# The third feed-forward quarter in two sets of seven block products, with the residual kept in DRAM

## What is computed

```python
def swiglu(x, w_gate, w_up, w_down):
    return (jax.nn.silu(x @ w_gate) * (x @ w_up)) @ w_down

h = h + 0.5 * rmsnorm_2(swiglu(u, ff1_w_gate, ff1_w_up, ff1_w_down), ff1_post_g)   # and again with ff2
```

## Time and profile before

| | us |
|---|---|
| median of three runs | 2805.66 |
| lowest and highest of them | 2805.01, 2805.68 |
| span of the profiled execution | 2803.9 |
| TensorE busy in it | 2789.1 |
| VectorE busy in it | 2219.1 |
| ScalarE busy in it | 1485.1 |

### The profile page before, as it was taken

One profiled execution on the slowest core, in us unless ns is written; L12 is line 12 of the kernel. 1 busy time (PEld: TensorE's weight loads), 2 busy tenths in 40 slices (PEclk: granted clock), 3 DMA queues, 4 the chain that ended last, 5 costly groups with the idle time before them and its releaser, 6 DMA issues.

```text
span 2803.9 us, 34346 instructions
## 1 busy us (share of the span) xinstructions
PE 2789.1 (99%) x13154; PEld 2329.8 (83%) x13154; DVE 2219.1 (79%) x2554; ACT 1485.1 (53%) x1747; POOL 14.5 (1%) x20
## 2 busy tenths in 40 slices
PE   9999999999999999999999999999999999999998
PEld 8888888888898888888888888888888888888887
DVE  6869757865565888889888877687799888889885
ACT  5544545554544555555455555755655555555564
POOL 0000000000000000000000000000000000000000
PEclk9999999999999999999999999999999999999999
DMA  7546355555545555655655558543665656565654
GB/s 250 202 155 199 112 182 190 186 189 180 165 150 197 196 193 197 206 199 199 202 196 194 196 165 270 177 160 125 204 200 189 203 187 208 197 204 198 204 187 158
DMA packets 276010, 530.71 MB, mean 189 GB/s; under 512 B 8769, under 2 KB 32465, under 8 KB 275393
## 3 DMA queue, kind: packets, MB, share of 16 engines
q1 hardware_dynamic: 274864, 527.01, 56.6%
q0 software_dynamic: 752, 2.04, 0.2%
q10 hardware_dynamic: 288, 0.20, 0.0%
HBM read 527.12 MB, written 2.10 MB: 189 GB/s over the span
## 4 chain that ended last, share of the span: by engine, by line
PE 97%; DVE 1%; DMA 0%; ACT 0%; issue 0%; SPq 0%; DVEq 0%; ACTq 0%
PE ps L817 19%; PE ps L818 19%; PE ps L820 17%; PE ps L1373 10%; PE ps L1375 9%; PE ps L1374 9%; PE ps L826 2%; PE ps L902 1%; PE ps L901 1%; PE ps L900 1%; PE ps L845 1%; PE ps L846 1%; PE ps L850 1%; PE ps L1081 1%; PE ps L1367 1%; PE ps L1061 1%
## 5 line engine op out<-in xcount | busy, mean ns | idle before, releaser
L2450 DVE TENSOR_TENSOR w_lo<-raw,w_hi 128x2048 fp32r<-128x2048 f32 (+4 forms) x301 | 663.0, 2206 | 193.9 <-ACT w_hi L1683 193.1
L1683 ACT ACTIVATE w_hi<-raw 128x2048 fp32r<-128x2048 f32 (+4 forms) x301 | 555.1, 1849 | 259.5 <-DMA raw<-in_ff_w_down 107.4
L817 PE MATMUL ps<-w_hi,x_hi 128*128 128x512 f32 (+4 forms) x1760 | 679.1, 386 | 1.7 <-ACT z L1716 0.7
L818 PE MATMUL ps<-w_lo,x_hi 128*128 128x512 f32 (+4 forms) x1760 | 669.5, 380 | 0.0
L820 PE MATMUL ps<-w_hi,x_lo 128*128 128x512 f32 (+4 forms) x1536 | 582.7, 379 | 0.0
L817 PEld LDWEIGHTS ps<-w_hi,x_hi 128*128 128x128 f32 x1760 | 330.7, 188 | 62.6 <-issue 2.3
L818 PEld LDWEIGHTS ps<-w_lo,x_hi 128*128 128x128 f32 x1760 | 330.9, 188 | 58.6
L820 PEld LDWEIGHTS ps<-w_hi,x_lo 128*128 128x128 f32 x1536 | 288.4, 188 | 53.3
L2217 ACT ACTIVATE w_hi<-raw 128x1024 fp32r<-128x1024 f32 x156 | 164.9, 1061 | 278.4 <-DMA raw<-in_ff_w_up 144.7
L1373 PE MATMUL ps<-w_hi,x_hi 128*128 128x512 f32 x780 | 305.4, 392 | 0.1
L1375 PE MATMUL ps<-w_hi,x_lo 128*128 128x512 f32 x780 | 303.8, 389 | 0.0
(11 more groups left out here) (486 smaller groups left out, 4019.4 us busy)
## 6 DMA issues: line engine op xcount, KB each, us to landing
raw<-in_w_in SPq DMA_DIRECT2D x139, 1024.0 KB, 5.1
raw<-in_ff_w_gate SPq DMA_DIRECT2D x88, 1024.0 KB, 5.2
raw<-in_ff_w_up SPq DMA_DIRECT2D x88, 1024.0 KB, 5.3
raw<-in_ff_w_down SPq DMA_DIRECT2D x88, 1024.0 KB, 5.1
raw<-in_w_out SPq DMA_DIRECT2D x45, 1024.0 KB, 5.2
raw<-in_w_ple_gate SPq DMA_DIRECT2D x16, 1024.0 KB, 5.0
raw<-in_w_in SPq DMA_DIRECT2D x8, 696.0 KB, 4.3
raw<-in_w_in SPq DMA_DIRECT2D x8, 520.0 KB, 3.8
```

What stands on the lines that cost most here:

```text
L817: nc.tensor.matmul(o, x[0][:, k0 + c, s], hi[:, c, 0:width], start=first and c == 0, stop=False)
L818: nc.tensor.matmul(o, x[0][:, k0 + c, s], lo[:, c, 0:width], start=False, stop=False)
L1683: nc.scalar.activation(landed_part(w_hi, u, j), landed_part(raw, u, j), ACT.Copy).then_inc(hi_ready, 1)
L2450: V.tensor_tensor(landed_part(w_lo, u, j), landed_part(raw, u, j), landed_part(w_hi, u, j).bitcast(F32), ALU.subtract).then_inc(parts_read ...
```

## The change

Block i = 0 keeps its three sets. In the blocks i = 1 to 9 quarter 2 (`DOUBLE`) is done wholly in two sets of seven, so that a block has five sets: (0,0), (1,0), (2,0), (2,1), (3,0). The sums of activations for the new set (`half_xs`, lower and upper part) are made once in block 0, in memory of attention masks.

The sums now are four chunks apart from the units: up - gate for both chunks in one instruction of 1024 columns (`first_sums`), then two of 512. There is a second place for them in the memory of `res`, used by the sets (1,0) and (2,1) from block 1 on. For that POOL writes `res` to a DRAM tensor at the start of each feed-forward, VectorE waits for the end of this write before block 1, and SP reads it back in four parts between the last four down loads.

The upper part of a gate unit is one instruction of 2048 columns (it was two of 1024), that of an up unit one of 1536 (1024 in the double quarter), those of the sums two of 1024. The lower parts are 1024 (plain gate), 1024 (gate), 1536 (up) and 2048 (sums) columns; in the double quarter 2048 (gate), 1024 (up) and twice 2048. The lower parts of gate units overwrite `raw`, and wait for all sums of the quarter.

TensorE's order changes: in quarters 1 and 3 the plain up half stands last; in quarter 0 the gate's own products come late, and both units are given free together; in the double quarter the gate's own products come first. The silu is made in place, and the additions of the gate and of the up sums are two steps that no longer wait for each other.

The diff, cut to its core:

```diff
 TensorE: summed_pair
+                    if p == DOUBLE and sets is SETS:
+                        pe.wait_ge(parts_ready, u + 1)
+                        gate_products(0)
+                        gate_products(1).then_inc(parts_used, 1)
+                        pe.wait_ge(sums_ready, n + 1)
+                        sums(0, (4, 5, 7, 3)).then_inc(sums_used, 1)
+                        pe.wait_ge(parts_ready, u + 2)
+                        up_product(0)
+                        up_product(1).then_inc(parts_used, 1)
+                        pe.wait_ge(sums_ready, n + 2)
+                        sums(1, (4, 5, 7, 3)).then_inc(sums_used, 1)
+                        return
...
+                    pe.wait_ge(plain_gate_ready, plains_before(no, i) + (singles.index(p) + 1))
                     plain(2, gate)
+                    if p == 0:
                         between()
+                        pe.wait_ge(parts_ready, u + 2)
                         plain(0, up)
+                        up_product(0)
+                        pe.wait_ge(sums_ready, n + 1)
+                        sums(0, (4, 5, 3))
+                        before_rest()
+                        gate_products(0).then_inc(parts_used, 2)
+                        sums(0, (7,)).then_inc(sums_used, 1)
+                        return
...
 VectorE
+                def first_sums(u, i, p, h=0):
...
+                    dve.wait_ge(raw_landed[j], u * 4 + (16 - 4 * j))
+                    dve.wait_ge(raw_landed[j + 1], u * 4 + (16 - 4 * j))
+                    if not isinstance(n, int) or n > held:
+                        dve.wait_ge(sums_used, n - held)
+                    c = 2 * h * BW
+                    V.tensor_tensor(ff_sums[sums_place(i, p, h)][:, 0:2],
+                                    raw[:, j + 1, c:c + 2 * BW].rearrange("p (k n) -> p k n", k=2),
+                                    raw[:, j:j + 2, c:c + BW], ALU.subtract).then_inc(sums_made, 1)
...
+                def gate_lo(u, i, p, c=slice(0, 2)):
...
+                    dve.wait_ge(hi_ready, u + 1)
+                    dve.wait_ge(sums_made, n * 3 + (6 if (p, 1) in sets else 3))
+                    lo(chunks(c), 2 * p % RAW).then_inc(parts_ready, 1)
...
+                def pair_lo(u, i, p, beside=None):
...
+                        first_sums(u, i, p)
+                        plain_gate_lo(u, p)
+                    second_sum(i, p, 1)
+                    third_sum(i, p, 2)
+                    gate_lo(u, i, p)
+                    sums_lo(i, p)
+                    up_lo(u, i, p)
+
+                def double_lo(u, i, p):
+
+                    first_sums(u, i, p, 0)
+                    first_sums(u, i, p, 1)
+                    second_sum(i, p, 1, 0)
+                    second_sum(i, p, 2, 1)
+                    third_sum(i, p, 3, 0)
+                    third_sum(i, p, 4, 1)
+                    gate_lo(u, i, p, slice(0, UC))
+                    sums_lo(i, p, 0)
+                    up_lo(u, i, p)
+                    sums_lo(i, p, 1)
...
 SP, the last down units
-                down4(u0 + 12 * FB - 4, FB - 1)
+                sp.wait_ge(sums_used, (FF1, FF2).index(b) * SETS_ALL + SETS_ALL - 1)
+                for j in range(4):
+                    c = slice(j * BW, (j + 1) * BW)
+                    load(u + j, j, slot(j, UC, BW), down[(FB - 1) * BW:FB * BW, c].rearrange("(k p) n -> p k n", p=P))
+                    sp.dma_start(res[:, :, c], kept_res[:, :, c]).then_inc(res_back, 16)
...
 POOL, at the start of each feed-forward
+            pool.dma_start(kept_res, res[:]).then_inc(res_kept, 16)
```

More of the change, by code:

```diff
@@ new lines, in sums @@
+                    def sums(h, banks):
+                        place = sums_place(i, p, h)
+                        w = lambda m: [t[:, m] for t in (ff_sums_hi[place], ff_sums_lo[place])]
+                        for bank in banks:
+                            if bank == 4:
+                                k = three(4, xsum(h, 0), w(0), first, last)
+                            elif bank == 5:
+                                k = three(5, xsum(h, 1), w(2), first, last)
+                            elif bank == 7:
+                                k = three(7, xsum(h, 2), w(1), first, last)
+                                if last:
+                                    k.then_inc(shared_done, 1)
+                            else:
+                                k = three(3, x(2 * h + 1, 1), w(3), False, p == 3)
+                        return k
@@ new lines, in gate_products, with up_product @@
+                    def gate_products(h):
+                        three(6, x(2 * h, 0), of(gate, 2 * h), first, last)
+                        return three(2, x(2 * h + 1, 0), of(gate, 2 * h + 1), False, p == 3)
+                    def up_product(h):
+                        return three(0, xsum(h, 3), of(up, 2 * h + 1))
+                    if first and sets is SETS_FIRST:
+                        pe.wait_ge(xs_ready, (xs_before(no) + 1) * len(xs_runs))
+                    if p == DOUBLE and sets is SETS:
[10 more added lines that the diff above has]
+                        return
@@ L1408, in summed_pair @@
+                        sums(0, (7,)).then_inc(sums_used, 1)
+                        return
                     if before_rest:
                         before_rest()
-                    pe.wait_ge(parts_ready, u + 1)
-                    three(6, x(0, 0), of(gate, 0), first, last)
-                    three(2, x(1, 0), of(gate, 1), False, p == 3).then_inc(parts_used, 1)
-                    pe.wait_ge(parts_ready, u + 2)
-                    m = three(7, xsum(2), of(up, 0), first, last)
-                    if last:
-                        m.then_inc(shared_done, 1)
@@ L1417, in summed_pair @@
-                    m = three(0, xsum(3), of(up, 1))
-                    if p == 3:
-                        pe.wait_ge(plain_ready, n * 2 + 2)
-                        m = plain(0, up)
-                    m.then_inc(parts_used, 1)
+                    if p == 3:
+                        pe.wait_ge(parts_ready, u + 1)
+                        gate_products(0).then_inc(parts_used, 1)
+                    pe.wait_ge(sums_ready, n + 1)
+                    sums(0, (4, 5, 7, 3)).then_inc(sums_used, 1)
@@ L1423, in down @@
+                    if p < 3:
+                        pe.wait_ge(parts_ready, u + 1)
+                        gate_products(0).then_inc(parts_used, 1)
+                    pe.wait_ge(parts_ready, u + 2)
+                    up_product(0)
+                    plain(0, up).then_inc(parts_used, 1)
                 def down(u, i, last=None):
@@ new lines, in sums_lo @@
+                def sums_lo(i, p, h=0):
+                    place = sums_place(i, p, h)
+                    sets = sets_of(i)
+                    hi_before = 2 * (sums_before(no, i) + sets.index((p, 0)))
+                    dve.wait_ge(sums_hi_ready, hi_before + (2 if (p, 1) not in sets else 3 + h))
+                    V.tensor_tensor(ff_sums_lo[place][:], ff_sums[place], ff_sums_hi[place][:].bitcast(F32),
+                                    ALU.subtract).then_inc(sums_ready, 1)
+                def pair_lo(u, i, p, beside=None):
+                    if beside:
+                        plain_gate_lo(u, p)
+                        beside()
+                        first_sums(u, i, p)
+                    else:
+                        first_sums(u, i, p)
+                        plain_gate_lo(u, p)
+                    second_sum(i, p, 1)
[3 more added lines that the diff above has]
+                    up_lo(u, i, p)
```

299 lines of the change are left out of this document (171 added, 128 removed).

## The result

| | before | after |
|---|---|---|
| median of the runs, us | 2805.47 | 2926.58 |
| lowest and highest, us | 2805.01, 2805.68 | 2925.09, 2927.94 |
| span of the profiled execution, us | 2803.9 | 2923.3 |

The changed kernel is slower by 4.3%: the ratio is 1.0432, with a 95% interval of 1.0419 to 1.0445. Forecast were 2884 us, with a range from 2862 to 2910.

The account below looks back on a forecast made before the run. TensorE was taken to bound the kernel. From a span of 2803.9 us: -12.2 (matmuls) + 83.7 (stalls) + 1.7 (block 0) + 5 (clock) = 2882.1; with the median 1.8 above the span, 2884 us, range 2862 to 2910.

Parts of the forecast that it names:

- the bound: Feed-forward: TensorE bounds the kernel, busy 2789.1 of 2803.9 us, with everything else hidden.
- the saving: Quarter 2 of blocks 1 to 9: 54 TensorE matmuls fewer over both feed-forwards, 12.2 us.
- the chain: Quarter 0's unit release, loads, sums, gate_lo: ends 14.8 us after quarter 1's start against 10.20; 18 stalls of 4.65, 83.7 us.
- quarter 3: Blocks 1 to 9: plain_gate_lo ready 1.5 us ahead of TensorE, so no wait.
- the residual's reads: Four 0.5 MB reads between the last down loads: at most 1.3 us each, taken as 0.
- the third rival: VectorE late again at quarter 3; with 1.5 us of delay 2911 us; chance 0.08.
- the first: Rival: the chain is covered by loads released sooner or landing faster; 2793 to 2795 us; chance 0.12.
- the clock's term: Matmuls behind the 18 stalls slowed by the clock falling to 1.2 GHz; a fifth of the upper bound taken, 5 us.
- the upper end: Clock falls in each of 18 stalls, six matmuls at half speed, 1.4 us a stall, 25 us.
- the second rival: The clock falls in nearly every double-quarter stall; 2904 us; chance 0.18.
- block 0: Quarter 1's sums due after four block products, not eight: 0.85 us late, twice, 1.7 us.
- The cover that the prediction named: First block products: ScalarE waits for loads, TensorE a unit or more behind, hiding the residual's write; 0 to 11 us, taken 0.

Follow-up runs that it names:

- the twenty matmuls: The changed kernel with 20 more matmuls ahead of TensorE's wait in each double quarter, filling the stall; 2891.15 us, ratio 1.0306 against the kernel before.
- the run with the residual alone: The kernel before plus the residual's write to DRAM and its four reads back, the freed SBUF place unused; 2805.97 us, ratio 1.0004.
- the run with the write put off: Five sets, early release, split double quarter; in block 0 gate products ahead of sums and residual write delayed to quarter 2; 2825.04 us, ratio 1.0073.
- The experiment without the fifth set: The changed kernel with the double quarter made a single one of 15 block products, all else kept; 2859.05 us, ratio 1.0189 against the kernel before.
- the early release: The changed kernel without the fifth set, plus quarter 0 reordered to free its units 2.7 us earlier; 2819.35 us, ratio 1.0053 against the kernel before.
- the one with block 0 eased: Same run as the run with the write put off; 2825.04 us, ratio 1.0073 against the kernel before.
- the kernel with the early release: The changed kernel, five sets kept, with gate and up products ahead of the sums in quarter 0; 2847.82 us, ratio 1.0150 against the kernel before.
- the sums on GpSimd: The one with block 0 eased, with the double quarter's second set's three sums moved from VectorE to GpSimd; 2883.96 us, ratio 1.0283 against the kernel before.

## Why the prediction was right and wrong

**Right: the bound, the saving and the chain.** The 54 matmuls went. The chain held at each link. With quarter 1 starting at 1393.28 (10.20 us ahead of 1403.48, its end), the issues, the landings on ScalarE and VectorE's part are:

```profile
1393.04 0.37 SPq L668 DMA_DIRECT2D raw<-in_ff_w_gate  x1
1393.60 0.37 SPq L668 DMA_DIRECT2D raw<-in_ff_w_up  x1
```

```profile
1398.20 1.92 ACT L2311 ACTIVATE w_hi<-raw 128x2048 fp32r<-128x2048 f32 x1 [5.49 <-DMA raw<-in_ff_w_gate]
1400.85 1.06 ACT L2316 ACTIVATE w_hi<-raw 128x1024 fp32r<-128x1024 f32 x1 [0.73 <-DMA raw<-in_ff_w_up]
```

```profile
1400.91 1.22 DVE L3380 TENSOR_TENSOR z<-raw 128x1024 f32<-128x1024 f32 x1 [4.16 <-issue]
...
1405.71 2.29 DVE L3360 TENSOR_TENSOR w_lo<-raw,w_hi 128x2048 fp32r<-128x2048 f32 x1
1407.92 2.29 DVE L3420 TENSOR_TENSOR ws_lo<-z,ws_hi 128x2048 fp32r<-128x2048 f32 x1
```

The issue is at -0.24 (forecast -0.23), the up unit lands 7.81 us after the gate's issue (7.89 from the earlier trace rows) and 2.65 us behind the gate unit though asked for only 0.56 us behind it: the transfers are in line, as read. From 1400.91 to 1407.92 are 7.0 us (7.1). Reading two units at a stride costs nothing: 1.22 us, as any 1024 columns. VectorE stands idle for 4.16 us ahead of it with nothing to do: it is late, not overloaded. The stalls are 4.46 us on the mean, 80.3 us against 83.7. With TensorE kept busy in them, so that only the clock is taken out, a steady block takes 67.51 us, against the 67.8 forecast; in the change it takes 69.61.

**Right: quarter 3, the down part and the residual's reads.** No wait for them stands among TensorE's waits; the third rival did not happen, nor the first: the up unit landed four microseconds too late for it.

**Wrong: the size of the clock's term.** This is the step that put the time out of the range: 5 us taken, 25 at the upper end, 37.6 read in the rows and 35.4 taken off by the twenty matmuls. Two things failed in it. The likely value: I let a fifth of the stalls fall, and all 18 did. The Trainium skill's rule named in the prediction (TensorE: Matmul & The Clock Gate, HAM oscillation: the clock is down at every burst) held for every stall of this length. And the upper end: six slow matmuls a stall, where there are 7 to 14; so the second rival, which is what happened, was priced too low as well, at 2904 us, with 1.4 us a stall for 2.1. The prediction said that no row shows matmuls at the lower level. That was false. The trace of before has them, behind the very wait of 1.7 us that the earlier trace rows show:

```profile
1624.60 0.51 PE L845 MATMUL ps<-w_hi,x_hi 128*128 128x512 f32 x1 [1.71 <-ACT x_hi L1888]
...
1627.04 0.63 PE L845 MATMUL ps<-w_hi,x_hi 128*128 128x512 f32 x1
1627.47 0.63 PE L846 MATMUL ps<-w_lo,x_hi 128*128 128x512 f32 x1
...
1629.84 0.48 PE L845 MATMUL ps<-w_hi,x_hi 128*128 128x512 f32 x1
```

```profile
1625.00:1626.00 1.00, 1.00 (x6) 0.82 (x5) 0.52 (x1) 0.00 (x0) 0.00 (x0) 0.50 1.04 395
```

What this fall cost can be read without a model, because the run with the residual alone has the same wait and the same matmuls, and there the granted clock stayed at 1.00:

```profile
1625.70 0.47 PE L856 MATMUL ps<-w_hi,x_hi 128*128 128x512 f32 x1 [1.71 <-ACT x_hi L1899]
...
1629.35 0.48 PE L856 MATMUL ps<-w_hi,x_hi 128*128 128x512 f32 x1
```

From the first matmul behind the wait to the next group of products are 5.24 us before and 3.65 us there: the fall cost 1.6 us. I had looked for the clock at the end of the run, where nothing follows, and not behind the one wait in the middle. With 1.6 us a stall the sum would have been 2882 - 5 + 29 = 2906 us of span, 2908 us: inside the range, and still 19 us short. Of these 19, 9 us are that a fall cost 2.1 us on the mean and not 1.6, because in 7 of the 18 stalls the clock fell early and 2.7 to 3.0 us were lost; another 8 us are block 0.

**Wrong: block 0.** 1.7 us were forecast, and it was 6.3 + 2.0 of waits and 1.5 of clock. The estimate let first_sums start at 972.09; it started at 974.97. The up unit was taken up by ScalarE at 957.41 before and at 960.30 after:

```profile
957.41 1.92 ACT L1683 ACTIVATE w_hi<-raw 128x2048 fp32r<-128x2048 f32 x1 [3.51 <-DMA raw<-in_ff_w_up]
```

```profile
960.30 1.92 ACT L1777 ACTIVATE w_hi<-raw 128x2048 fp32r<-128x2048 f32 x1 [5.57 <-DMA raw<-in_ff_w_up]
```

```profile
974.97 1.22 DVE L3380 TENSOR_TENSOR z<-raw 128x1024 f32<-128x1024 f32 x1
```

Its load was issued at 952.07 before and at 951.99 after, the same; the write of the residual was issued from POOL's queue at 947.41, and 2 MB beside the loads held this one back by 2.9 us. VectorE's later steps are all later by as much. The cover that the prediction named, TensorE being a unit or more behind the loads, was there in the kernel before, as the residual alone shows, and not here, because block 0 of the change needs its sums four block products earlier: it was used up by another part of the same change, 2.3 of the 3.2 us. That it is the write that delays the load is shown by the run of the residual alone, where nothing else was changed: from issue to take-up are 8.4 us there and 8.3 in the change, 5.3 in the kernel before, and 5.1 again in the run with the write put off (952.48 to 957.58), where first_sums starts at 972.28, within 0.2 us of what the prediction had. How the 3.2 us of the wait divide is an estimate: that run moved the gate products too.

**Not foreseen: the single sets' own stall.** The experiment without the fifth set shows that quarter 2 would stand still with four sets as well. The prediction saw the late release and the late place of gate_lo as the fifth set's price; without the fifth set the change is 54 us slower all the same. That is no share of the 121 us, since the double quarter takes the place of the very quarter that stands still there; with the early release these waits went, and 15 us were left. The same sum, landing 7.7 and work 7.1 against 10.20 + 2.72, would have given it.

No kernel of the study is faster than the one before. The nearest with five sets, the one with block 0 eased, takes 63.82 us for a steady block, still 0.2 us above the kernel before, and loses most in and around block 0.

## What to carry to other kernels

Where a tuned kernel is bound by one engine, work out for each unit of data the chain release, transfer, preparation, first use, and hold it against the time until that use: an order that uses the prepared data first, or frees a buffer later, takes slack out of the chain at both ends, and here 12 us of saved matmuls cost 80 us of waiting. Price a stall of TensorE with the slow matmuls behind it too, and look for that price behind a wait that the trace already has, however short and wherever it lies; here such a wait gave 1.6 us where the new, longer stalls cost 2.1. Work that is hidden alone must be held against the new due times of the change, not against the old ones.

## What the runs showed of the hardware

- The clock after a wait. It fell behind every one of the 18 waits of 4.1 to 4.7 us. Behind shorter ones it was either: in the kernel without the fifth set, behind 3 of 18 waits of 1.5 to 1.8 us (1.7 us lost each), in the kernel with the early release behind none of 16 of 1.5 to 1.9 us; with the sums on GpSimd behind 13 of 18 waits of 2.3 to 4.6 us; in the changed kernel behind one of 3.19 us and not behind one of 3.07 us; behind the same wait of 1.71 us in the kernel before and not in the run with the residual alone. What tells these apart I could not read from the rows. A fall cost 1.4 to 3.0 us beyond the wait, 7 to 14 matmuls at 0.43 us, and most where the clock had fallen 0.67 us or more before the matmuls came back.
- A VectorE instruction with two SBUF inputs took 2.78 us for 0.69 while GpSimd worked on SBUF. A GpSimd instruction on 1024 columns took 2.78 us there, one on 512 columns 1.6.
- Two loads of 1 MB issued 0.56 us apart landed 2.65 us apart, the same as two issued 1.10 us apart before.
- A write of 2 MB to DRAM, issued from POOL's queue 4.6 us ahead of a load of 1 MB, made that load take 8.3 to 8.4 us from issue to take-up in place of 5.1 to 5.3.
